# Loading head 0 of the attention during the projection before it, and moving the cached steps one head later

## What is computed

```
qa, ka, va, fa, ga, qb, kb, vb, iq, ik, iw, gb = split_cols(h @ w_in, AB_COLS)
oa = fox_block(qa, ka, va)      # softmax(q k^T/8 + cum_f[query] - cum_f[key], causal) v
ob = dsa_block(qb, kb, vb)      # softmax over the 256 keys that the indexer picked (top_k) v
mixed = concat([oa * silu(ga), ob * silu(gb)]) @ w_out
x = x + gate * mixed
```

## Time and profile before

| | us |
|---|---|
| median of 3 runs | 1955.83 |
| lowest, highest | 1950.13, 1958.43 |
| the profiled execution, whole | 1954.82 |
| its span in the profile | 1953.1 |

### The profile page before, as it was taken

The page is one execution under the profiler, slowest core; times in us unless marked ns, Lnnn a source line. Parts: engine busy times, 40 slices in busy tenths (PEclk is TensorE's granted clock), DMA queues, the critical chain, the costliest instruction groups (busy, mean ns, idle before and its releaser), DMA issues. The chain is left out here.

```text
span 1953.1 us, 34285 instructions
## 1 busy us (share of the span) xinstructions
PE 1697.0 (87%) x12683; PEld 1325.5 (68%) x12754; DVE 1300.7 (67%) x2849; ACT 942.5 (48%) x1897; POOL 240.0 (12%) x339
## 2 busy tenths in 40 slices
PE   5696679999998975899998997979996999899798
PEld 2462458888876864677776786767784767677686
DVE  2633577887999943678888654562455777777764
ACT  4401452226411263677876224437644766777421
POOL 4101100000000002101110000000004222221000
PEclk7696799999999997899998998989997999999899
DMA  8365612432232219968774542242225111111442
GB/s 293 136 208 185 107 58 71 128 110 87 76 92 77 101 49 217 230 193 222 195 203 145 216 181 98 67 125 94 76 73 113 35 28 45 27 27 51 151 130 97
DMA packets 229742, 235.18 MB, mean 120 GB/s; under 512 B 139797, under 2 KB 164661, under 8 KB 227530
## 3 DMA queue, kind: packets, MB, share of 16 engines
q1 hardware_dynamic: 218778, 198.91, 36.1%
q0 software_dynamic: 10800, 34.08, 4.6%
HBM read 173.98 MB, written 58.95 MB: 119 GB/s over the span
## 5 line engine op out<-in xcount | busy, mean ns | idle before, releaser
L352 PE MATMUL PS<-ab_wh,hT 128*128 128x512 f32 x576 | 231.8, 403 | 5.7 <-DVE ab_wl L697 5.7
L353 PE MATMUL PS<-ab_wl,hT 128*128 128x512 f32 x576 | 227.1, 394 | 0.0
L354 PE MATMUL PS<-ab_wh,hT 128*128 128x512 f32 x576 | 226.8, 394 | 0.0
L1190 DVE TENSOR_SCALAR_CACHE_REDUCE topk_junk<-scores,topk_small 128x528 bf16<-128x528 f32 (+6 forms) x224 | 194.6, 916 | 1.3
L2365 DVE CUSTOM_DVE_ANT_0 la_S<-PS,la_mask 128x128 f32<-128x128 f32 (+3 forms) x144 | 107.6, 747 | 41.5 <-PE PS L354 28.5
L352 PEld LDWEIGHTS PS<-ab_wh,hT 128*128 128x128 f32 x576 | 109.4, 190 | 28.7 <-ACT ab_wh L625 3.9
L354 PEld LDWEIGHTS PS<-ab_wh,hT 128*128 128x128 f32 x576 | 109.3, 190 | 25.3
L1540 ACT ACTIVATE at_P<-at_S,at_nm 128x128 f32<-128x128 f32 (+2 forms) x144 | 110.5, 767 | 30.7 <-DVE at_nm L1585 30.5
L353 PEld LDWEIGHTS PS<-ab_wl,hT 128*128 128x128 f32 x576 | 109.4, 190 | 22.2
L352 PE MATMUL PS<-out_wh,out_mT 128*128 128x512 f32 x288 | 116.4, 404 | 4.7 <-DVE out_mT L1813 4.7
L2287 ACT ACTIVATE la_P<-la_S,la_nm 128x128 f32<-128x128 f32 (+3 forms) x144 | 110.4, 767 | 9.3 <-DVE la_nm L2365 9.2
(11 more groups left out here) (426 smaller groups left out, 4499.5 us busy)
## 6 DMA issues: line engine op xcount, KB each, us to landing
ab_wl_raw<-in_ab_w_in SPq DMA_DIRECT2D x64, 256.0 KB, 5.2
out_g<-scratch_gates_nat SPq DMA_DIRECT2D x18, 512.0 KB, 5.8
mod_ada_w<-in_ada_w SPq DMA_DIRECT2D x8, 1024.0 KB, 13.2
mod_w<-in_ada_w SPq DMA_DIRECT2D x16, 512.0 KB, 6.1
mod_w<-in_ada_w SPq DMA_DIRECT2D x8, 1024.0 KB, 6.7
at_kc<-in_cache_a_k SPq DMA_DIRECT2D x8, 1024.0 KB, 9.1
at_vc<-in_cache_a_v SPq DMA_DIRECT2D x8, 1024.0 KB, 7.5
at_kc<-in_cache_b_k SPq DMA_DIRECT2D x8, 1024.0 KB, 7.9
```

The costliest lines, as they stand in the source:

```text
L352: nc.tensor.matmul(out, x[0], w[0], start=start, stop=False)
L353: nc.tensor.matmul(out, x[0], w[1], start=False, stop=False)
L354: return nc.tensor.matmul(out, x[1], w[0], start=False, stop=stop)
L1190: go(V.tensor_scalar(mark, x, limit, 0.0, op, ALU.add, accum_out=cnt[:, m:m + 1]), 0 if m == M - 1 else 1)
```

## The change

1. Head 0's q, k and v are loaded by SP during the projection, at step 54 (the first tile of the seventh group), by a new object `FirstHead`; q and v lie in the buffer `mod2_bias`, k in a new one. In the attention, head 0 then has only its decay row to load.
2. A head's q comes in one DMA, whose source has the dimensions 2, 64 and 1024, and its k in two of 64 x 2 x 1024; before, they were six of 64 x 1024.
3. The batch step of chunk l stands after head l+1; batches 14 and 15 both stand at the end. Their loads and POOL's addition move along.
4. In the projection the groups gate b (silu) and vb (copy) change places, so that vb is last.
5. Two buffers move from one side of SBUF to the other.

```diff
@@ projection: SP, in the loop over steps
+                if first_head and s == 6 * NT:
+                    sp.wait_ge(nat_done, 3 * NT + 5)
+                    first_head.load(sp)
                 if s < len(steps) and steps[s][1] == 1:
                     load_weights(sp, steps[s][0] + 1)
@@ new functions
+def load_head_rows(sp, c, x, h, q, k, arrived):
+    queries, keys = (c.s["qaT"], c.s["kaT"]) if x == 0 else (c.s["qbT"], c.s["kbT"])
+    sp.dma_start(q, dram(queries, h * DH * TOK, [[HD * TOK, 2], [TOK, DH], [1, SEQ]])).then_inc(arrived, 16)
+    for half in range(2):
+        sp.dma_start(k[DH * half:DH * (half + 1)], dram(keys, h * DH * TOK, [[TOK, DH], [HD * TOK, 2], [1, SEQ]])).then_inc(arrived, 16)
+class FirstHead:
+        self.q, self.v = free[:, 0:512].bitcast(BF16), free[:, 512:1024].rearrange("p (j d) -> p j d", d=DH)
+        self.k = stack.enter_context(nc.sbuf_tensor("at_k0", [P, 2, SEQ], BF16, side="right"))
+    def load(self, sp):
+        load_head_rows(sp, self.c, 0, 0, self.q, self.k, self.head_in)
+        load_values(sp, self.c, 0, 0, self.v, self.v_in)
@@ branches_ab
     for g in range(G):
-        order += [("head", g, i) for i in range(QT)] + [("batch", g, QT)]
+        order += [("head", g, i) for i in range(QT)] + ([("batch", g - 1, QT)] if g else [])
+    order.append(("batch", G - 1, QT))
...
-            for g in range(G):
-                for half in range(2):
-                    sp.dma_start(q[DH * half:DH * (half + 1), g % 3, :], qT[x][half, h * DH:(h + 1) * DH, 0:SEQ]).then_inc(head_in[g % 3], 16)
-                    for d in range(2):
-                        sp.dma_start(k[DH * half:DH * (half + 1), g % 3, d, :], kT_dram[x][d, h * DH:(h + 1) * DH, 0:SEQ]).then_inc(head_in[g % 3], 16)
+                if g:
+                    load_head_rows(sp, c, x, h, q(g), k(g), head_in[g % 3])
...
+            load_head(0)
+            load_head(1)
+            stage_rows(0)
+            load_batch(0)
+            sp.dma_start(c.s["mask_s"], c.score(QT)).then_inc(mask_out, 16)
+            for g in range(2, G):
+                load_head(g)
+                load_batch(g - 1)
+            load_batch(G - 1)
@@ POOL, in the loop over g
-                if g < H:
-                    pool.wait_ge(add_in[g % 2], 16 * (g // 2 + 1))
+                l = g - 1
+                if 0 <= l < H:
+                    pool.wait_ge(add_in[l % 2], 16 * (l // 2 + 1))
@@ build
-                      ab(b0 + 2 * HD, HD, "copy", nat("b_v"), None, None),
-                      ab(x0 + HD + DH + H, HD, "silu", gates(HD), None, None)]
+                      ab(x0 + HD + DH + H, HD, "silu", gates(HD), None, None),
+                      ab(b0 + 2 * HD, HD, "copy", nat("b_v"), None, None)]
```

More of the change, by code:

```diff
@@ L64 @@
     f"out{l}_{m}{n}" for l in range(2) for n in range(2) for m in ("stored", "row")] + ["out0_w_in0", "out0_w_in1", "out0_g_in0"] + [
-    f"ab_w_in{k}" for k in range(KT)]
+    f"ab_w_in{k}" for k in range(KT)] + ["at_head_in0", "at_v_in0"]
 def store_semaphore(name):
@@ L479, in __init__, with projection @@
         self.nat, self.turned, self.scale, self.keep, self.slot = nat, turned, scale, keep, slot
-def projection(nc, c, name, groups, idle=None, pair=BF16, ring=4, side=None, front=None, weights=None, sums=None):
+def projection(nc, c, name, groups, idle=None, pair=BF16, ring=4, side=None, front=None, weights=None, sums=None, first_head=None):
     S = lambda n: semaphore(nc, f"{name}_{n}")
@@ L1252, in selection, with load_values, __init__, branches_ab @@
     return idle
-def branches_ab(nc, c, out):
+def load_head_rows(sp, c, x, h, q, k, arrived):
[3 more added lines that the diff above has]
+        sp.dma_start(k[DH * half:DH * (half + 1)], dram(keys, h * DH * TOK, [[TOK, DH], [HD * TOK, 2], [1, SEQ]])).then_inc(arrived, 16)
+def load_values(sp, c, x, h, v, arrived):
+    rows = c.o["p_a_v" if x == 0 else "p_b_v"][0, 0].rearrange("t h d -> t (h d)")[:, h * DH:(h + 1) * DH]
+    sp.dma_start(v, rows.rearrange("(j p) n -> p j n", p=P)).then_inc(arrived, 16)
+class FirstHead:
+    def __init__(self, nc, c, stack, sums):
+        self.c = c
+        self.head_in, self.v_in = store_semaphore("at_head_in0"), store_semaphore("at_v_in0")
+        free = sums.bias[:].rearrange("p a b -> p (a b)")
+        self.q, self.v = free[:, 0:512].bitcast(BF16), free[:, 512:1024].rearrange("p (j d) -> p j d", d=DH)
[3 more added lines that the diff above has]
+        load_values(sp, self.c, 0, 0, self.v, self.v_in)
+def branches_ab(nc, c, out, first_head):
     S = lambda n: semaphore(nc, f"at_{n}")
@@ L1260, in branches_ab @@
     for g in range(G):
-        order += [("head", g, i) for i in range(QT)] + [("batch", g, QT)]
+        order += [("head", g, i) for i in range(QT)] + ([("batch", g - 1, QT)] if g else [])
+    order.append(("batch", G - 1, QT))
     N = len(order)
-    head_at = lambda g, i: (QT + 1) * g + i
-    batch_at = lambda l: (QT + 1) * l + QT
+    place = {(kind, g, i): s for s, (kind, g, i) in enumerate(order)}
+    head_at = lambda g, i: place["head", g, i]
+    batch_at = lambda l: place["batch", l, QT]
     tiles_done = lambda g, i: QT * g + i + 1
@@ L1355, in _ @@
-                if g >= 2:
-                    sp.wait_ge(maxed, batch_at(g - 2) + 1)
-                if g == H:
-                    sp.wait_ge(mask_out, 16)
[L1359 to L1363, removed]
@@ L1364, in _, with load_batch @@
-                sp.dma_start(vc[:, g % 2], cache_v[x][0, h].rearrange("(j p) h d -> p j (h d)", p=P)).then_inc(vc_in[g % 2], 16)
-                sp.dma_start(vn[:, g % 2, :], new_v[x][0, h].rearrange("t h d -> t (h d)")).then_inc(vc_in[g % 2], 16)
+                if g:
+                    load_values(sp, c, x, h, v(g), v_in[g % 2])
+            def load_batch(l):
+                x, b = l // H, l % H
+                if l == 2:
+                    stage_rows(1)
+                if l >= 2:
+                    sp.wait_ge(turned, number["keys", l - 2, NP - 1] + 1)
+                sp.dma_start(kc[:, l % 2], cache_k[x][0, b].rearrange("(j p) h d -> p j (h d)", p=P)).then_inc(kc_in[l % 2], 16)
+                if l >= 2:
+                    sp.wait_ge(maxed, batch_at(l - 2) + 1)
+                if l == H:
+                    sp.wait_ge(mask_out, 16)
+                rows = (dram(c.s["negcum_s"], b * H * KEYS, [[KEYS, H], [0, TS], [1, KEYS]]) if x == 0 else
+                        dram(c.s["mask_s"], b * TS * KEYS, [[0, H], [KEYS, TS], [1, KEYS]]))
+                sp.dma_start(addt[:, l % 2], rows).then_inc(add_in[l % 2], 16)
+                if l >= 2:
+                    sp.wait_ge(turned, number["value", batch_at(l - 2), 0] + 1)
+                sp.dma_start(vc[:, l % 2], cache_v[x][0, b].rearrange("(j p) h d -> p j (h d)", p=P)).then_inc(vc_in[l % 2], 16)
+                sp.dma_start(vn[:, l % 2, :], new_v[x][0, b].rearrange("t h d -> t (h d)")).then_inc(vc_in[l % 2], 16)
@@ L1434, in score_head @@
                     for d in range(2):
-                        last = nc.tensor.matmul(PS[:, to + a // 512, 0:w], q[:, g % 3, i * P:(i + 1) * P], k[:, g % 3, d, a:a + w],
+                        last = nc.tensor.matmul(PS[:, to + a // 512, 0:w], q(g)[:, i * P:(i + 1) * P], k(g)[:, d, a:a + w],
                                                 start=d == 0, stop=d == 1 and not masked_end)
@@ L2480, in build @@
             index_scores(nc, c, sums, weights)
+            first_head = FirstHead(nc, c, score_stack, sums)
             retire_semaphores(nc)
@@ L2495, in build @@
                 c.topk.small = inner.enter_context(nc.sbuf_tensor("topk_small", [P, 9, len(SELECT_TILES) + 1], F32))
-                projection(nc, c, "ab", groups, selection(nc, c), weights=weights)
+                projection(nc, c, "ab", groups, selection(nc, c), weights=weights, first_head=first_head)
             retire_semaphores(nc)
```

35 lines of the change are left out of this document (15 added, 20 removed).

## The result

| | before | after |
|---|---|---|
| median of 17 runs, us | 1955.62 | 1963.07 |
| lowest, highest | 1950.05, 1959.99 | 1960.02, 1968.64 |
| span of the profiled execution | 1953.1 | 1965.1 |
| last store of the projection issued | 726.93 | 727.22 |
| first maximum of the attention on DVE | 743.08 | 739.00 |

The ratio of the times is 1.0043 (95% interval 1.0033 to 1.0054): slower by 7.5 us. Up to the attention's first maximum the kernel is 4.1 us ahead; in the attention it loses 14.2. The two profiled executions differ by 12.0 us, the medians by 7.5; 1.9 of the 12.0 lie behind the attention, in stages that are the same. (The times of a place come from the profiled execution of each kernel. `at_masked` is what DVE writes of each batch step.

The account below looks back on a forecast made before the run. PE was taken as the bound in the projection and further on in the attention. The terms 4.2 - 5.5 - 3.7 - 5.4 - 3.9 + 2 + 6 gave -6.3, so a median of 1949.5 us, range 1936 to 1972.

Parts of the forecast that it names:

- The late split: Projection's last group: its last weight piece comes late, PE stands 2.5 us, then a lower clock costs 1.7; +4.2, bounds 0 and 6.
- The stage's end: End of the projection: with the copy kind last, the last store follows PE by 0.9 instead of 6.4 us; -5.5.
- head 0's loads: Start of the attention: six DMAs no longer stand ahead of the decay row that sets DVE's start; -3.7.
- kc -5.4: Early attention: batch 0's keys are wanted eight steps later, so PE's stall on kc goes; -5.4, bounds 0 and -7.4.
- the addition -3.9: Batch 0: DVE's wait for POOL's addition, which followed a late v, goes; -3.9, bounds 0 and -3.9.
- the end +2: Attention's tail: batch 14 no longer fills head 15's small first tiles and batch 15 follows directly; +2, bounds 0 and +4.
- The q transfer: Attention's loads: q on two DMA engines delays batch 0 by some 5 us, plus 1 later; +6, bounds -1 and +54.
- the slower rival: Heads 1 to 15: two DMA engines become the bound of the attention; +33, so 1976 us; chance 0.26.
- a rest of -12.3: Whole kernel: the sum if the q transfers cost nothing, giving 1943.5 us; that case had chance 0.28.
- PE idle less than 3 us in 905 to 1007: Sign in the attention's window 905 to 1007 us: PE idle this little would refute the slower rival.
- batches of branch b lay 18 us or more apart: Sign in the attention's branch b: this spacing would make the prediction wrong; 17.0 us apart or more was expected.

Follow-up runs that it names:

- e4: The changed kernel with POOL's addition to addt ahead of the split of the next head's v: 1963.46 us, ratio 1.0037 to before.
- e1: The changed kernel with a head's q again in two transfers of 64 rows: 1931.09 us, 0.9883 of before.
- e6: e1 with each batch step again after its own head, loads and POOL's addition with it: 1947.07 us, ratio 0.9956 to before.
- e12: The kernel before with its six q and k transfers per head replaced by e10's three interleaved ones of 128 partitions: 1939.01 us, 0.9918 of before.
- e11: e10 with three instead of four selection pieces per DVE step in the projection's seventh group: 1914.06 us, 0.9788 of before.
- e3: The kernel before with only gate b and vb changing places in the projection: 1954.18 us, ratio 0.9995 to before.
- e10: The changed kernel with q's and k's partitions interleaved, q in one and k in two transfers to 128 partitions: 1919.4 us, 0.9821 of before.
- e13: e11 with POOL's addition ahead of the next split: 1917.0 us, 0.9810 of before.
- e2: The kernel before with only q in one transfer with 2 outermost: 1968.56 us, ratio 1.0070 to before.

## Why the prediction was wrong

The forecast was 1949.5, faster by 6; the kernel became slower by 7.5. Step by step:

- *The late split, +4.2:* right in mechanism and time (end at 678.86 for 678.6), too small in size: the last group takes 7.3 us more, beyond the bound of 6. PE came 1.4 us sooner to the split, so it stood 4.28 us for 2.5, and the lower clock cost 3.0 for 1.7. In the eight kernels with this projection code the group took 54.2 to 54.5 us in six and 56.5 and 56.7 in the other two (after and e4), against 49.2 before: 5 us in most and 7 in this one.
- *The stage's end, -5.5, and head 0's loads, -3.7:* right. Store 0.9 us behind PE; DVE's start 11.8 us behind the last store, where it was 16.2, that is -4.4.
- *kc -5.4, the addition -3.9, the end +2, together -7.3:* the order of the batches is worth 16 in the fair comparison (e1 with e6). Two of the terms were there, 7.8 us. What I left out is the work behind a wait at the lower clock: I priced that for the split and not here, and in e6 against e1 it is 11.8 of the 18.4 us.
- *The q transfer, +6: this step failed.* It costs 32 us (after with e1). Its mechanism was written down, its upper bound (+54) held, and the slower rival gave +33 for it. I took 6 because "later the loads have one to two heads of lead" and because two engines alone should run nearer the best rate. Both arguments fail. The lead did not last: all through the attention a v's last step came 7 to 10 us behind its fourteenth. And 5.6 MB in 331 us are 17 KB a us, near the mean and not 25, if the two never rest. Batches 1 to 7 lay 18.9 to 20.4 us apart, 7 to 10 16.6 to 17.1, and 10 to 13 18.6, 18.0 and 18.1; the late ones are about the 17.5 to 20 that I had worked out.
- The slower rival's time, 1976, was 13 too high for the other reason: it stood on a rest of -12.3 that was -24.5. So the forecast had two terms too small, with opposite signs (+6 for 32, -12.3 for -24.5), and it missed by 13.6 us and not by 26 because they partly cancel: that is luck. The rival also had PE's own pauses come more often; the changed kernel has none of over 1 us.

Two signs that I had named were clear. PE idle less than 3 us in 905 to 1007 would refute the slower case; it was idle 7.7. And the prediction was to be wrong if batches of branch b lay 18 us or more apart, as three in a row do.

## What to carry to other kernels

Before a transfer is merged with others to save issues, look at the outermost dimension of its source: 2 there put 256 KB per head on two of sixteen DMA engines and cost 32 us, more than the rest of the change gave, though the mean DMA share went down. A row without a time to landing is a mark of it. When a shared resource paces a stage, removing the longest wait in the profile can change nothing (e4), and other gains do not show until the resource is free. Price a wait of PE with the slower matmuls behind it. A transfer that fills 128 partitions, with a permuted order where the contraction allows it, gave 15.7 us in the kernel before and 11.7 beyond e1.

## What the runs showed of the hardware

- The number of DMA engines went with the outermost dimension of the source: 2, 4 and 16 gave 1963.1, 1940.6 and 1925.7 us for the same bytes, and two, four and none of the sixteen steps of the v behind it came late (with 2, the fourteenth step at 5.4 us and the sixteenth at 14.3).
- A transfer of q made 3, 5 and 16 steps of its semaphore with 2, 4 and 16 outermost, and `at_addt` 9 with 8.
- With q and k in transfers to 128 partitions the engines moved 19.6 KB a us while busy in branch b (e12), with those to 64 partitions 16.6 (before); it was 15.7 us of the kernel.
- After a wait of 4.28 us TensorE did 35 matmuls in the 10 us from 680 instead of 46 (e11), at a granted clock of 0.75. With a wait of 2.70 us the last group took 3.0 us more than without (52.2 for 49.2, e3, its clock at 1.00), with waits of 3.5 us 5 more, with waits of 4.3 and 4.6 us 7.3 and 7.5 more.
- The pauses of over 1 us on PE that no semaphore explains numbered four in before and e6 and none in e10, e11 and e13, with a mean DMA share of 0.69 to 0.70 over the attention. But e12 had two at 0.68, and after, e2 and e4, where two engines carry q, none at 0.68 to 0.72. Their cause was not measured.
